# Input-projection evictions on ScalarE, adaLN units spread over row tiles, dense stages begun inside the norms, and changed orders at stage ends

## The chip, the cores and the metric

One core of a Trainium2 chip runs the whole program in one launch. The metric is the device time in microseconds (us) of one execution, as the median of several. Engines: TensorE (PE; weight loads are PEld), VectorE (DVE), ScalarE (ACT), GpSimd (POOL) and SyncE (SP), which here issues loads. Each engine runs its own program in order and waits on semaphores.

## What is computed

A two-layer backbone over 512 latent and 256 context rows (six row tiles of 128; NT = 6, LT = 4 latent tiles) of width 1024, in float32. Cut to what matters:

```python
for layer in range(2):                                   # 0 even, 1 odd
    mod = silu(c) @ ada_w[layer] + ada_b[layer]          # adaLN: 6 x 1024, for c and for c_ctx
    h = rms_norm(x, pre_mix_g) * (1 + mod[1]) + mod[0]
    p = h @ w_in                                         # even 1184 columns, odd 2560
    a, b = (mla(p), swa(p)) if layer == 0 else (na(p), gqa(p))   # some columns RMS-normed, some rotated
    x = x + mod[2] * rms_norm(concat(a, b) @ w_out, post_mix_g)
    h = rms_norm(x, pre_ffn_g) * (1 + mod[4]) + mod[3]
    gate, val = split(h @ ffn_up)                        # 2 x 2816 columns
    f = (gelu(conv3(gate)) * val) @ ffn_down
    x = x + mod[5] * rms_norm(f, post_ffn_g)
```

The context rows go through layer 0 wholly and through layer 1 only as keys and values.

## The kernel before, in words

**Products.** A float32 operand is split in a high part (ScalarE copies it to the rounded type, `split_hi`, L1159) and a low part (VectorE subtracts, `minus_hi`, L1424). Each product is three matmuls (`three`, L723 to 725; up projection L1056). Weights come in units: SP loads a unit into one of two raw slots, ScalarE and VectorE split it (`w_hi_done`, `w_lo_done`), PE uses it. Six PSUM banks hold accumulators, one per row tile; banks 6 and 7 are a ring that transposes (`turn`) and adaLN products share. `t_done`/`t_free` count its rounds, and a round waits until the one two before is emptied.

**Stages.** They follow one another: norm0, input projection in0 (72 to 228 us of the trace), MLA (`attention`, to 363), SWA (to 454), out0, norm1 (to 545), up0 (to 932), down0 (to 1112), norm2, in1 (to 1327), NA, GQA (to 1484), out1, norm3 (to 1553), up1 (to 1796), down1 (to 1929), norm4.

**Input projection** (PE L839, ACT `projection_splits` L1209, DVE L1653 with `chunk` L1579, POOL L1980). Two weight units per column chunk, all row tiles for each (`unit_mm`, L811). VectorE alone empties the banks (L1595) into four stage slots, squares the columns to be normed, scales and rotates them, and after each tile runs a tiny copy (`mark`, L1649) that lets POOL store the tile. In the even layer two adaLN units (256 columns of `ada_w`, 1 MB each, two raw slots, `ada_mm`) follow each weight unit, 16 in all; VectorE adds the four partial rows of each (`ada_evac`, L1430: L1437). PE waits for its load at L737. The latents of chunk 0 are turned in chunk 2. SP loads two adaLN units, then a weight unit, in turn (L624).

**Attention.** SP loads heads once `stages_stored` says the projection's tiles are in memory; VectorE waits for the same at step k == 0.

**Output projection** (PE L1018, ACT L1296). Two units; `out_order` has tiles 0 and 1 go through unit 0 first, the others through both at once. ScalarE splits both units and then copies and squares the first half of every bank (`first_half`, L1204).

**Norm** (ACT L1164, DVE L1526, POOL L1965). A loop over row tiles in four stages; VectorE releases a bank, makes the normed rows (L1509) and the low part of the turned rows (L1424). `late(0)` and `late(1)` split the next stage's first two weight units, at t == T and after the loop. PE turns each tile (`norm_turn` L785, `norm_turns` L793). Beside norm0 and norm2 PE runs the next projection's first unit tile by tile; beside norm1 and norm3 it only turns.

**Up projection** (PE L1038, ACT L1313, DVE L1804). 22 products of 96 matmuls, 128 gate and 128 value columns each, over banks 0 to 2 or 3 to 5. ScalarE and VectorE make the convolution, gelu and gate of a product and split the next unit. In layer 0 VectorE also multiplies a unit of layer 1's `ada_w` by both streams and sums it (`ada_multiply` L1468: L1478, L1481), PE sums that over partitions (`ada_across` L762, L767), and VectorE evacuates the row (`late_evac` L1443, L1449). 24 units go so: 22 in the up projection, unit 0 ahead of its first tile, two more in the down projection.

**Down projection** (PE L1073, ACT L1341, DVE L1843). Two column halves of eleven units. In the second half the last four (18, 20, 21, 19: `LATE_ORDER`) are done tile by tile, so that banks end one after another; units 20 and 21 are loaded after 19. POOL stores the table of relative-position biases (`toeplitz`, L2077) after the adaLN row of unit 21.

## Time and profile before

| | us |
|---|---|
| median of 3 runs (lowest, highest) | 1939.31 (1936.67, 1942.23) |
| the profiled execution, its own time | 1940.28 |
| its span, first to last instruction | 1938.6 |
| PE busy (x9850 matmuls) | 1736.3 (90%) |
| DVE, ACT, POOL busy | 1081.6, 598.9, 260.1 |
| chain that ended last: PE, DVE, DMA, ACT, issue | 70%, 13%, 5%, 4%, 4% |
| mean granted TensorE clock | 0.953 |
| store of the bias table (POOL, 3.8 MB), its queue's share, 975 to 1040 us | 37.1% |

Busy times overlap between engines. A share of the chain says what the end hung on. The stages lie one behind another, so that idle time of PE within one is read from that stage. In rows by time, the bracket holds the idle time before the instruction and what ended it.

### The profile page before, as it was taken

Reading aid. Unit: us, or ns where it says so; the run is one execution under the profiler, and the core shown is the slowest. Engines: PE = TensorE matmul, PEld = TensorE weight load, DVE = VectorE, ACT = ScalarE, POOL = GpSimd, SP = SyncE. Lnnn points to the kernel's source line nnn. Section 1 sums busy time; section 2 is a strip of 40 time slices with the busy share of each in tenths; the row PEclk is TensorE's granted clock in tenths of the full one; section 3 lists DMA queues with packets and bytes.
Section 4 is the critical chain, followed back from the end, with each engine's and each line's share of the span. In section 5 each row is a group of like instructions: output and inputs, shape, how many; then the busy total and the mean of one; then the engine's idle time right before and its main releaser. Section 6 shows DMA issues by size and latency. Waiting matters only on the chain.

```text
span 1938.6 us, 26920 instructions
## 1 busy us (share of the span) xinstructions
PE 1736.3 (90%) x9850; PEld 1378.1 (71%) x9850; DVE 1081.6 (56%) x2143; ACT 598.9 (31%) x941; POOL 260.1 (13%) x396
## 2 busy tenths in 40 slices
PE   5788599899889999999889978997989699999996
PEld 1667366567678888888667767885667578888785
DVE  3576555573667777777445473367743534443344
ACT  2201255562422211222224331113642333332342
POOL 0232223231200000000000020115521100000000
PEclk9899799999989999999999988998999899999998
DMA  8446923114333444334162533335502333332224
GB/s 288 140 163 225 242 44 87 25 26 131 122 107 103 124 130 129 105 114 130 65 132 80 179 124 131 115 113 133 134 19 84 123 87 87 108 87 76 76 98 141
DMA packets 258266, 224.15 MB, mean 116 GB/s; under 512 B 67484, under 2 KB 218411, under 8 KB 258178
## 3 DMA queue, kind: packets, MB, share of 16 engines
q1 hardware_dynamic: 249156, 202.50, 34.6%
q0 software_dynamic: 7008, 18.79, 3.3%
q10 hardware_dynamic: 2016, 1.71, 0.3%
q8 instruction: 54, 0.88, 0.2%
q14 instruction: 32, 0.26, 0.0%
HBM read 193.71 MB, written 29.25 MB: 115 GB/s over the span
## 4 chain that ended last, share of the span: by engine, by line
PE 70%; DVE 13%; DMA 5%; ACT 4%; issue 4%; POOL 2%; SPq 1%; DVEq 0%; ACTq 0%
PE ps L1056 32%; PE ps L723 7%; PE ps L724 7%; PE ps L725 7%; PE ps L900 5%; PE ps L982 4%; PE ps L945 4%; DMA w_raw<-in_ffn_down 2%; DVE act_lo L1424 1%; DVE w_lo L1424 1%; DVE late_row L1437 1%; DVE arena L1595 1%; PE ps L937 1%; PE ps L779 1%; DVE arena L1550 1%
## 5 line engine op out<-in xcount | busy, mean ns | idle before, releaser
L723 PE MATMUL ps<-w_hi,act_hi 128*128 128x512 f32 (+2 forms) x952 | 376.4, 395 | 45.2 <-DVE act_lo L1424 32.0
L1424 DVE TENSOR_TENSOR w_lo<-w_raw,w_hi 128x2048 fp32r<-128x2048 f32 (+3 forms) x114 | 209.5, 1839 | 299.0 <-ACT w_hi L1159 286.6
L724 PE MATMUL ps<-w_lo,act_hi 128*128 128x512 f32 (+2 forms) x952 | 372.8, 392 | 0.0
L725 PE MATMUL ps<-w_hi,act_lo 128*128 128x512 f32 (+2 forms) x952 | 372.6, 391 | 0.0
L1159 ACT ACTIVATE w_hi<-w_raw 128x2048 fp32r<-128x2048 f32 (+3 forms) x110 | 172.2, 1567 | 495.9 <-PE ps L725 352.0
L1056 PE MATMUL ps<-act_hi,w_hi 128*128 128x512 f32 (+1 forms) x1056 | 322.1, 359 | 2.8 <-DVE act_lo L1424 2.8
L1056 PE MATMUL ps<-act_lo,w_hi 128*128 128x512 f32 (+1 forms) x1056 | 322.9, 360 | 0.0
L1056 PE MATMUL ps<-act_hi,w_lo 128*128 128x512 f32 (+1 forms) x1056 | 319.6, 357 | 0.0
L723 PEld LDWEIGHTS ps<-w_hi,act_hi 128*128 128x128 f32 x952 | 185.4, 195 | 87.0 <-issue 40.7
L725 PEld LDWEIGHTS ps<-w_hi,act_lo 128*128 128x128 f32 x952 | 184.3, 194 | 35.9
L724 PEld LDWEIGHTS ps<-w_lo,act_hi 128*128 128x128 f32 x952 | 184.7, 194 | 34.7
L1056 PEld LDWEIGHTS ps<-act_hi,w_hi 128*128 128x128 f32 x1056 | 174.1, 189 | 37.9 <-issue 4.7
L1056 PEld LDWEIGHTS ps<-act_hi,w_lo 128*128 128x128 f32 x1056 | 176.2, 190 | 32.0
L1056 PEld LDWEIGHTS ps<-act_lo,w_hi 128*128 128x128 f32 x1056 | 175.2, 190 | 28.9
L900 PE MATMUL ps<-ident,arena 128*128 128x128 f32 x882 | 141.3, 290 | 28.4 <-ACT arena L1238 13.5
L900 PEld LDWEIGHTS ps<-ident,arena 128*128 128x128 f32 x882 | 97.2, 144 | 77.3 <-issue 30.5
L1326 ACT ACTIVATE arena<-ps,conv 128x768 f32<-128x768 f32 (+1 forms) x44 | 39.0, 886 | 345.2 <-PE ps L1056 319.1
L2055 POOL TENSOR_SCALAR arena<-arena,rinv 128x768 f32<-128x768 f32 (+3 forms) x144 | 111.6, 775 | 236.0 <-DVE rinv L1756 235.9
L1478 DVE SCALAR_TENSOR_TENSOR arena<-arena,silu 128x256 f32<-128x256 f32 x336 | 137.2, 479 | 0.9
L1255 ACT ACTIVATE arena<-arena,nb 128x768 f32<-128x768 f32 (+4 forms) x144 | 115.4, 801 | 28.1 <-DVE nb L1751 27.5
L1238 ACT ACTIVATE arena<-ps 128x384 f32<-128x384 f32 (+2 forms) x179 | 78.2, 437 | 143.9 <-PE ps L900 141.6
L1820 DVE SCALAR_TENSOR_TENSOR arena<-ps,conv,arena 128x511 f32<-128x511 f32 x66 | 41.6, 658 | 128.9 <-ACT arena L1326 128.9
(117 smaller groups left out, 1722.2 us busy)
## 6 DMA issues: line engine op xcount, KB each, us to landing
arena<-in_ada_w SPq DMA_DIRECT2D x44, 1024.0 KB, 9.5
w_raw<-in_ffn_up SPq DMA_DIRECT2D x88, 512.0 KB, 5.2
w_raw<-in_ffn_down SPq DMA_DIRECT2D x88, 256.0 KB, 2.9
w_raw<-in_odd_w_in SPq DMA_DIRECT2D x20, 512.0 KB, 4.6
arena<-mods SPq DMA_DIRECT2D x16, 512.0 KB, 7.2
proj_odd<-arena POOLq DMA_DIRECT2D x26, 256.0 KB, 2.4
x_after_mix<-arena SPq DMA_DIRECT2D x10, 512.0 KB, 2.9
arena<-x_after_mix SPq DMA_DIRECT2D x10, 512.0 KB, 4.3
```

The lines of the kernel that those rows point to most:

```text
L723: mm(out_, s_hi, m_hi, start=start, stop=False)
L724: mm(out_, s_hi, m_lo, start=False, stop=False)
L725: return mm(out_, s_lo, m_hi, start=False, stop=stop)
L900: last = nc.tensor.transpose(bank(b)[:, n * P:(n + 1) * P], src, ident[:, :])
L945: last = mm(out_of(x, off, n), qt[s][h, rows], kt[s][h, keys], start=True, stop=not rope)
L1056: last = mm(o, wt[:, k, :], m[:, k, rows], start=st, stop=sp_)
L1159: A(w_hi[:, s, 0:n], w_raw[:, s, 0:n], ACT.Copy).then_inc(w_hi_done, 1)
L1238: A(dst, bank(6, n * P), ACT.Copy).then_inc(left_free, 1)
L1255: A(dst, src, ACT.Exp, bias=nb[:, s, x:x + 1], scale=-1.0, accum_out=rsum[:, s, x:x + 1])\
L1424: V.tensor_sub(out_, full, hi.bitcast(fp32)).then_inc(sem_, 1)
L1478: ins = V.scalar_tensor_tensor(out=ada_sum[:, v, :], in0=w, scalar=x, in1=ada_sum[:, v, :], op0=ALU.mult, op1=ALU.add)
L2055: Q.tensor_scalar(v, v, rinv[:, k % 2, x:x + 1], 1.0, ALU.mult, ALU.mult).then_inc(p_scaled, 1)
```

## The change

Every engine's program is edited at the same seams.

- In both input projections ScalarE empties the banks (`evict`), squares included; VectorE only finishes tiles that are normed or rotated (`finish`), POOL stores the others straight from the stage slot; there are seven slots and no `mark`.
- The 16 adaLN units of in0 have three slots and go one at a time behind row tiles: `ADA_AT` maps (weight unit, tile) to them. SP issues weight units ahead of them.
- `first_half` in the output projections runs before the second split; the last two tiles of `out_order` go through unit 0 and then unit 1.
- In the norms the two late splits move to the start of iterations T-1 and T. PE does the first two up products in pieces of two row tiles (`rows_product`) between the turns, and both units of chunk 0 of in1 (`IN1_START`).
- In up0 `ada_multiply` runs at the end of a tile, unit 0 behind tile 0, and `ada_across` follows one product later. The last product does its low rows of weights first (`last_product`), so that the first half of G is split during it; down0's first unit takes banks by `up_banks`.
- In the down projections units 20 and 21 are loaded at the start of the second half and split before 17, 18 and 19; the first two and the last two tiles of the late units are interleaved.

Storage, placement and orders:

```diff
+STAGES = 7
...
-        stage = [plain(512) for _ in range(4)]
+        stage = [plain(512) for _ in range(4)] + [arena[:, 8704 + i * 512:9216 + i * 512] for i in range(3)]
+        early_raw = [ada_raw[:, 0], ada_raw[:, 1], arena[:, 4608:4608 + 2048].rearrange("p (k c) -> p k c", k=KC)]
...
+        ADA_AT = {(1, 5): [0, 1], (2, 1): [2], (2, 3): [3], (2, 5): [4], (3, 1): [5], (3, 3): [6], (3, 5): [7],
+                  (4, 5): [8], (5, 2): [9], (5, 5): [10], (6, 2): [11], (6, 5): [12], (6, 8): [13], (6, 11): [14],
+                  (7, 3): [15]}
+        TURN0 = 8
...
-        LATE_ORDER = [18, 20, 21, 19]
-        SPLIT_PLACE = {18: 20, 19: 21, 20: 18, 21: 19}
+        SPLIT_PLACE = {20: 17, 21: 18, 17: 19, 18: 20, 19: 21}
+        def late_order(T):
+            first = [(t, n) for t in range(2) for n in (20, 21, 18)] + [(t, 19) for t in range(2)]
+            middle = [(t, n) for t in range(2, T - 2) for n in (18, 20, 21, 19)]
+            return first + middle + [(t, n) for pair in ((18, 20), (21, 19)) for t in (T - 2, T - 1) for n in pair]
...
+            first, last = ([(t, n) for n in range(2) for t in ts] for ts in ((0, 1), (T - 2, T - 1)))
+            return first + [(t, n) for t in range(2, T - 2) for n in range(2)] + last
...
+        IN1_START = [("turn", 3), (0, 0), (0, 1), (0, 2), (1, 0), ("turn", 4), (1, 1), (1, 2), ("turn", 5), (0, 3), (1, 3)]
```

SyncE's loads (`early_unit(i)` loads adaLN unit i of the projection into slot i % 3 once unit i - 3 is summed); in the down projection `half` is the second half:

```diff
+                            sp.wait_ge(t_free, ada_round(0, ADA_FIRST + 14) + 1)
...
-            for n in range(8):
-                for g in range(ADA_FIRST + 2 * n, ADA_FIRST + 2 * n + 2):
-                    sp.wait_ge(t_free, ada_round(0, g - 2) + 1 if g - 2 >= ADA_FIRST else WIDES)
-                    ada_unit(0, g, g % 2)
-                k_unit(n + 2, *units[n + 2])
+            sp.wait_ge(t_free, WIDES)
+            for i in range(2):
+                early_unit(i)
+            for n in (2, 3):
+                k_unit(n, *units[n])
+            sp.wait_ge(h_ready, base("norm0", "h") + NT)
+            early_unit(2)
+            for n, late in ((4, (3, 4)), (5, (5, 6, 7)), (6, (8, 9)), (7, (10, 11)), (8, (12, 13)), (9, (14, 15))):
+                k_unit(n, *units[n])
+                for i in late:
+                    early_unit(i)
...
-                        if layer == 0:
-                            wait_apart(sp, (t_free, i * 2 + (base(up, "t") + k + 1)))
-                            ada_unit(1, i * 2 + (k + 2), k)
-                run_loop(sp, 0, FT // 2 - 1, up_trip)
+                        if layer == 0 and not (isinstance(i, int) and i == k == 0):
+                            wait_apart(sp, (t_free, i * 2 + (base(up, "t") + k)))
...
+                    if half:
+                        sp.wait_ge(w_lo_done, w0 - 1)
+                        for n in (20, 21):
+                            down_unit(layer, 2 * (n - FT // 2), half, n % 2, 1024)
...
+                        sp.wait_ge(t_free, ada_round(1, FT - 3) + 1)
+                        ada_unit(1, FT - 1, 1)
                         for k in range(2):
+                            run_loop(sp, 1 + 2 * k, 3 + 2 * k, down_trip)
                             sp.wait_ge(t_free, ada_round(1, FT - 2 + k) + 1)
                             ada_unit(1, FT + k, k)
-                            run_loop(sp, 1 + 2 * k, 3 + 2 * k, down_trip)
```

TensorE:

```diff
+            def into_projection():
+                u = base("in1", "w")
+                for what, t in IN1_START:
+                    if what == "turn":
+                        norm_turn("norm2", t)
+                        continue
+                    weights(u + what)
+                    turned("norm2", t)
...
+                            if u == 4:
                                 pe.wait_ge(staged, b + 1)
-                                turn(t0 + 8 + b, t0 + 8 + b,
+                                turn(t0 + TURN0 + b, t0 + TURN0 + b,
                                      [mla_in[b][:, k * P:(k + 1) * P] for k in range(3)])
-                        unit_mm(u % 2, tiles, 4, cn, (act_hi, act_lo), 4 * n, n == 0, n == 1, after=after)
...
+                def rows_product(j, g):
+                    weights(U0 + j)
+                    for t in (2 * g, 2 * g + 1):
+                        turned(nm, t)
+                    for half in range(2):
+                        b = 3 * j + 2 * half if g < 2 else 3 * j + 1
+                        o = bank(b, 256, 256 * g) if g < 2 else bank(b, CTX, CTX * half)
+                        if b < T:
+                            pe.wait_ge(acc_evac, base(name, "ev") - T + b + 1)
+                        for k in range(KC):
+                            cols = slice(half * 1024 + k * P, half * 1024 + (k + 1) * P)
+                            last = three_moving(o, w_hi[:, j, cols], w_lo[:, j, cols],
+                                                *(m[:, k, g * 256:(g + 1) * 256] for m in (act_hi, act_lo)),
+                                                k == 0, k == KC - 1)
+                        if g == T // 2 - 1:
+                            last.then_inc(mm_done, 1)
...
+                def last_product(slot):
...
+                    b = 3 * slot
+                    for half in range(2):
+                        last = passes(half, range(KC // 2), bank(b + 2 * half), slice(0, LAT))
+                    if full:
+                        for half in range(2):
+                            last = passes(half, range(KC), bank(b + 1, CTX, CTX * half), slice(LAT, ROWS))
+                    last.then_inc(low_free, 1)
+                    for half in range(2):
+                        passes(half, range(KC // 2, KC), bank(b + 2 * half), slice(0, LAT)).then_inc(mm_done, 1)
...
-                    if full:
-                        ada_across(i * 2 + (base(name, "t") + k), k, i * 2 + (k + 1))
...
+                    if full and not ends:
+                        ada_across(i * 2 + (base(name, "t") + k - 1), 1 - k, i * 2 + k)
...
+                todo = [(j, g) for g in range(T // 2) for j in range(2)]
+                for t in range(T - 3, T):
+                    if T == NT:
+                        rows_product(*todo.pop(0))
+                    norm_turn(nm, t)
+                    if T == LT and t > T - 3:
+                        rows_product(*todo.pop(0))
+                for j, g in todo:
+                    rows_product(j, g)
+                if full:
+                    ada_across(base(name, "t"), 0, 1)
+                run_loop(pe, 1, FT // 2 - 1, lambda i: [tile(i, k, True) for k in range(2)])
+                tile(FT // 2 - 1, 0, True)
+                tile(FT // 2 - 1, 1, True, True)
...
+                def up_banks(b):
+                    if b in (0, 3):
+                        pe.wait_ge(gated, base(name, "f") - (b == 0))
...
+                        order = late_order(len(tiles))
+                        for i, (t, n) in enumerate(order):
+                            done = ends(order, t) == i + 1
+                            late(t, n, done)
+                            if nf == "norm2" and t >= 3 and done:
                                 norm_turn(nf, t - 3)
```

ScalarE (norm, input projection, output projection, last tile of the up projection, down projection):

```diff
-                    if t == T and late is not None:
-                        late(0)
+                    if T - 1 <= t <= T and late is not None:
+                        late(t - T + 1)
...
+                    other = 0 if c >= 3 and layer == 0 or n % 2 else 1 if layer and c == 0 else len(tiles)
+                    act.wait_ge(mm_done, in_done(layer, c, len(tiles) - 1) - other)
...
+                def evict(c):
+                    spec = IN_SPECS[layer][c]
+                    n = spec["n"]
+                    for x, t in enumerate(in_tiles(layer, c)):
+                        ev, st, _, nsq = in_counts(layer, c, x)
+                        act.wait_ge(mm_done, in_done(layer, c, x))
...
+                            last = A(scrap[:, off:off + w], bank(x)[:, at:at + w], ACT.Square, accum_out=ssh[:, p, k:k + 1])
...
+                            at_least(act, stage_out[st % STAGES], 16 * (st // STAGES))
+                            dst = stage[st % STAGES][:, 0:n]
+                        A(dst, bank(x, n), ACT.Copy).then_inc(acc_evac, 1)
...
+                    split(2 * c)
+                    if layer and c == 0:
+                        for s in range(2):
+                            act.wait_ge(x_st[s], 16 * base("in1", "xs") // 2)
+                    evict(c)
+                    split(2 * c + 1)
...
+                    if n:
+                        for t in range(T):
+                            act.wait_ge(mm_done, mm0 + T + t + 1)
+                            first_half(t)
...
-                act.wait_ge(mm_done, base(name, "mm"))
...
+                        act.wait_ge(low_free, layer + 1)
+                        for n in range(2):
+                            A(act_hi[:, 2 * n:2 * n + 2, 0:cols], G[:, 2 * n:2 * n + 2, 0:cols], ACT.Copy).then_inc(g_hi, 1)
...
+                if layer == 0:
+                    act.wait_ge(ada_summed, ADA_UNITS)
```

VectorE (norm, attention, up projection and its last tile, down projection):

```diff
+                    if T - 1 <= t <= T and late is not None:
+                        late(t - T + 1)
...
-                    if k == 0 and a.name in ("mla", "na"):
+                    if k < 0 and a.name in ("mla", "na"):
...
-                if full:
-                    ada_multiply(0, ADA_USES + 1)
...
-                        late_evac(i * 2 + (T0 + k), k, i + (ADA_USES + 1))
-                        ada_multiply(1 - k, i + (ADA_USES + 1 + k))
...
+                        if not (isinstance(i, int) and i == k == 0):
+                            late_evac(i * 2 + (T0 + k - 1), 1 - k, i + (ADA_USES + k))
+                        if ada == 1:
+                            ada_multiply(k, i + (ADA_USES + 1))
...
+                        for n in range(2):
+                            dve.wait_ge(g_hi, base(f"down{layer}", "g") + n + 1)
+                            chunks = slice(2 * n, 2 * n + 2)
+                            minus_hi(act_lo[:, chunks, 0:cols], G[:, chunks, 0:cols], act_hi[:, chunks, 0:cols], g_lo)
+                    tile(FT // 2 - 1, k, 1024, 2 * full if k == 0 else 0)
...
+                    ada_multiply(0, ADA_USES + FT // 2)
...
+                for first, last, g in ((0, 1, FT - 1), (1, 3, FT), (3, 4, None)):
+                    run_loop(dve, first, last, lambda i: [step(i, k, 0, 0) for k in range(2)])
+                    if g is not None:
+                        ada_turn(g)
```

GpSimd, in the input projection:

```diff
+                    if on_vector(layer, c, t):
+                        pool.wait_ge(staged, done + 1)
+                    else:
+                        pool.wait_ge(acc_evac, ev + 1)
```

## Rows read from the trace of the kernel before

**Rows 1.** Busy time by stage, all engines; us, (x) instructions

```profile
core 0: us, PE busy (x) PEld busy (x) DVE busy (x) ACT busy (x) POOL busy (x), PEclk, DMA share, GB/s
112.00:228.00 116.00, 84.56 (x564) 67.39 (x562) 79.38 (x203) 11.44 (x12) 26.29 (x49) 0.91 0.70 228
...
518.00:545.00 27.00, 15.22 (x73) 12.02 (x71) 22.37 (x25) 12.37 (x22) 4.11 (x11) 0.74 0.61 195
...
545.00:932.00 387.00, 386.38 (x2280) 327.66 (x2280) 278.61 (x585) 78.61 (x65) 11.44 (x21) 0.99 0.38 113
```

**Rows 2.** Waits of PE, 80 to 229 us: us in total, times, longest

```profile
PE ps L737 <- DMA late_bias<-in_ada_b: 14.9, 5, 6.3
...
PE ps L723 <- DVE arena L1595: 12.2, 5, 5.6
...
PE ps L900 <- DVE late_row L1437: 9.6, 1, 9.6
```

**Rows 3.** VectorE groups, 80 to 228 us; busy us, mean ns, idle before

```profile
L1437 DVE TENSOR_TENSOR late_row<-ps,late_row 2x256 f32<-2x256 f32 x48 | 20.2, 420 | 1.6
...
L1595 DVE COPY arena<-ps 128x512 f32<-128x512 f32 x18 | 12.4, 690 | 8.0 <-DMA mla_kv<-arena 7.8
```

**Rows 4.** ScalarE groups, 228 to 545 us; same columns

```profile
L1199 ACT ACTIVATE act_hi<-ps 128x512 fp32r<-128x512 f32 x12 | 6.9, 596 | 8.9 <-PE ps L779 8.9
```

**Rows 5.** Busy time in one 5 us stretch; columns of rows 1

```profile
130.00:135.00 5.00, 5.00 (x24) 4.14 (x23) 4.83 (x10) 0.00 (x0) 1.06 (x2) 1.00 1.04 344
```

**Rows 6.** PE by time, second pass of the first output projection

```profile
489.89 0.61 PE L723 MATMUL ps<-w_hi,act_hi 128*128 128x512 f32 x1 [3.18 <-ACT ps L1207]
```

**Rows 7.** PE by time, transposes at the end of the first post-mix norm

```profile
533.82 1.94 PE L779 MATMUL ps<-ident,arena 128*128 128x128 f32 x8 [4.85 <-DVE act_lo L1424]
```

**Rows 8.** Chain by time, first two up-projection products; start, us, what

```profile
545.62 19.60 PE ps L1056 x96
...
565.55 17.16 PE ps L1056 x96
```

**Rows 9.** VectorE by time, first two up-projection tiles

```profile
571.65 2.29 DVE L1424 TENSOR_TENSOR w_lo<-w_raw,w_hi 128x2048 fp32r<-128x2048 f32 x1 [0.55 <-ACT w_hi L1159]
...
575.60 5.75 DVE L1478 SCALAR_TENSOR_TENSOR arena<-arena,silu 128x256 f32<-128x256 f32 x14
...
589.15 2.29 DVE L1424 TENSOR_TENSOR w_lo<-w_raw,w_hi 128x2048 fp32r<-128x2048 f32 x1 [0.57 <-ACT w_hi L1159]
...
592.57 0.62 DVE L1481 TENSOR_SCALAR arena<-arena,silu 128x256 f32<-128x256 f32 x2
...
593.10 5.76 DVE L1478 SCALAR_TENSOR_TENSOR arena<-arena,silu 128x256 f32<-128x256 f32 x14
```

**Rows 10.** PE by time, even down projection

```profile
941.24 0.77 PE L723 MATMUL ps<-w_hi,act_hi 128*128 128x512 f32 x1 [8.79 <-DVE act_lo L1424]
...
987.61 0.40 PE L767 MATMUL ps<-arena,ones 128*1 128x128 f32 x8 [3.97 <-DVE arena L1478]
...
1018.84 0.57 PE L723 MATMUL ps<-w_hi,act_hi 128*128 128x512 f32 x1 [4.49 <-DVE act_lo L1424]
...
1107.47 0.47 PE L723 MATMUL ps<-w_hi,act_hi 128*128 128x512 f32 x1 [3.06 <-DVE act_lo L1424]
```

**Rows 11.** Chain by time, even down projection

```profile
1001.36 22.58 DMA w_raw<-in_ffn_down
```

**Rows 12.** DMA issues (page, part 6): KB each, median us from issue to landing

```profile
w_raw<-in_ffn_down SPq DMA_DIRECT2D x88, 256.0 KB, 2.9
```

**Rows 13.** VectorE by time, before the norm after it

```profile
1118.11 1.23 DVE L1462 SCALAR_TENSOR_TENSOR arena<-arena 128x1024 f32<-128x1024 f32 x1 [7.98 <-DMA arena<-in_pre_mix_g]
```

**Rows 14.** PE by time, odd input projection's start

```profile
1135.19 1.97 PE L779 MATMUL ps<-ident,arena 128*128 128x128 f32 x8 [4.10 <-DVE arena L1509]
...
1184.61 0.77 PE L723 MATMUL ps<-w_hi,act_hi 128*128 128x512 f32 x1 [4.96 <-DVE w_lo L1424]
```

**Rows 15.** PE by time, odd layer: norm, down projection, last units

```profile
1541.23 1.94 PE L779 MATMUL ps<-ident,arena 128*128 128x128 f32 x8 [7.04 <-DVE act_lo L1424]
...
1798.97 0.77 PE L723 MATMUL ps<-w_hi,act_hi 128*128 128x512 f32 x1 [3.74 <-DVE act_lo L1424]
...
1905.79 0.77 PE L723 MATMUL ps<-w_hi,act_hi 128*128 128x512 f32 x1 [6.20 <-DVE act_lo L1424]
```

588 lines of the change are left out of this document (286 added, 302 removed).

## Prediction

> **What bounds the kernel now.** I read the stages first. TensorE (PE) is busy nearly all the time in the even up projection (386.38 of 387 us) but not in the even input projection (84.56 of 116 us) or at the end of the first post-mix norm (15.22 of 27 us) [rows 1]. No other engine is near its limit: VectorE has 79.38 us of work in the 116, ScalarE 11.44 [rows 1]. So the time is PE's work plus PE's idle stretches, and the change is read stretch by stretch: what PE waits for there, and what waits last once that is gone. Next I read the waits of PE in the input projection: five on the loads of adaLN weights, 14.9 us; five on the bank evictions (line 1595), 12.2; one on the last adaLN row at attention's start, 9.6 [rows 2]. Last I read PE by time in the other stages. An idle stretch costs more than itself: the first up-projection product after the norm takes 19.60 us, the next 17.16 [rows 8], and the granted clock of the 27 us before is 0.74 [rows 1]. I add 1.0 to 2.4 us after an idle stretch of over 3 us and nothing after a shorter one.
>
> The sum is made against the profiled execution, 1940.3 us (its span is 1938.6); the median of the runs, 1939.3, is 1 us lower, which I leave out.
>
> **Input projection, even layer.** VectorE's 18 evictions of 512 columns (12.4 us) and the others move to ScalarE, which has the room. The price there: 596 ns for 128x512 from PSUM [rows 4] against VectorE's 690 [rows 3]. "ScalarE: Activation LUTs" of the Trainium skill (Rules for kernel authors) says to keep such simple operations on VectorE and budgets 0.3 us plus 0.83 ns an element for an activation; that is an estimate of 0.72 us and would make 26 such evictions 3 us longer than by the row, off the path as long as ScalarE is idle; the trace does not agree, and the sum goes by the row. The adaLN units no longer come in pairs after a weight unit but singly behind row tiles, three weight slots ahead; each costs VectorE four additions, 16 units x 4, the same as before (48 of them 20.2 us, [rows 3]). Placed by hand in the new order, PE runs from 86 us with waits of 1 to 2 us and ends its last tile near 178 instead of 219; SP then still issues the loads for attention one after another, and the first scores come about 40 us sooner. The 36.7 us of waits [rows 2] plus some 4 us of slow clock are there to be won. Against that stand the transfers: 116 us at 228 GB/s are 26.4 MB [rows 1], and the highest rate in view, 344 GB/s at a share of 1.04 [rows 5], moves them in 77 us, so this stretch can give 39 us at most and the 7.8 us of idle ahead of it a little more. I take **38**; bounds 27 (the loads' and evictions' waits alone) and 47. The wait for all stores is now ahead of the first score minimum instead of after it; VectorE, and with it the softmax of both first attentions, stands behind it. The stores land before the first scores are there, so it costs 0 (up to +3 at either attention).
>
> **Output projections.** ScalarE now empties each bank as it is finished instead of after the last split. PE's 3.18 us at 489.89 [rows 6] and the same wait in the odd layer go, with 0.7 and 1.4 of slow clock: **8.5**. The split of the second unit is then behind four to six evictions; PE has two tiles, over 5 us, before it needs it, so 0 to +1.
>
> **First norm into the up projection.** PE waits 4.85 us at 533.82 and twice more [rows 7]; the first product starts at 545.62 and the second ends at 582.7 [rows 8]. The six half-sized pieces are together the same 34.3 us and can begin once unit 0's low part is made. But VectorE now makes it (2.29 us, [rows 9]) ahead of the last tile's norm, which delays the turned rows by as much. By hand: pieces from 531.5, with three transposes between them, the last of product 0 done at 564, of product 1 at 569.5. That alone would be 13 us. Then PE meets the adaLN sum of unit 0. Before, VectorE made it ahead of the first tile; now behind it: product 0's end to unit 2's low part is 8.7 us (565.2 to 573.9), and 14 of the 16 multiply-adds are 5.75 us, so all about 6.5 [rows 8, 9]. PE is released 15.2 us after 564, at 579.2, and the third product begins there instead of at 583, with 2 us of slow clock: **2**. Bounds: -3 (if the norm slips more) and +13 (if that sum hid).
>
> **Up into down, even layer.** 8.79 us idle [rows 10]. Two of the four row chunks of the first unit are split before the last product ends, and the first three of six tiles need only the banks of the tile before. PE does about 4 us, waits 1.5 for the last gate, does the rest, and again waits for an adaLN sum that VectorE makes behind the last tile: some 3.5 us. **4.5** (0 to 10). In the middle, the 3.97 us on that sum [rows 10] go with their slow clock, 5.5. The 22.58 us landing of a weight load [rows 11], with the 4.49 us stall after it [rows 10], comes from the store of the bias table beside it. That store now starts later, among the loads of the second half, which have two units more in front. "DMA: Bandwidth & Descriptors" (SWDGE vs HWDGE vs iDMA) of the Trainium skill says an engine takes turns between the two kinds of queue; by that the load would only take about twice its 2.9 us [rows 12] and the stall be none, so that the middle would give 2.5 more than my term; the trace has 22.58, and I keep the stall and charge 2.5 for the worse place: **3** (-6 to +12).
>
> **Second norm into the odd input projection.** The 3.06 us before the last units [rows 10] go, but the norm cannot start until the gain row is loaded after the last split (7.98 us on that load, [rows 13]), so the stall at 1135.19 (4.10, [rows 14]) grows by as much. What is won comes after: tile 5's products end sooner, PE works on both halves of chunk 0 inside the norm, and the 4.96 us at 1184.61 [rows 14] fill up. By hand, chunk 0 ends at 1188 instead of 1197: **9** (0 to 14). At the end of the odd projection VectorE no longer lags by its own copies and squares: **3** (0 to 4).
>
> **Third norm into up.** Only four row tiles. PE waits 7.04 us at 1541.23 [rows 15]. Unit 0's low part now goes ahead of tile 3, the transposes queue behind the same two banks, and both products end together instead of 11 us apart, so unit 2's split starts late: third product at 1581.5 instead of 1577.6, **-4** (-6 to +8). **Odd down projection:** 3.74 us at 1798.97 with slow clock, **5**; 6.20 us at 1905.79 with slow clock, as the units 20 and 21 are loaded early, **8** of 21.8 us of last units (4 to 9) [rows 15].
>
> **Sum:** 38 + 8.5 + 2 + 4.5 + 3 + 9 + 3 - 4 + 5 + 8 = 77 us; 1940.3 - 77 = **1863**.
>
> **Rivals.** (A) The overlap in the norms is really won. For: PE's order allows it, and of 11 us at both up projections I give nearly all back to waits that I placed by hand. Against: rows 9. Then 13 instead of 2 and +3 instead of -4, and a calmer middle: 1843. Chance 0.2. (B) The input projection stays bound by transfers: average share 0.70 already [rows 1], saturated stretches [rows 5]. Then only some 20 us come there: 1881. Chance 0.2. (C) The overlaps fail and the store of the bias table stops the second half too; only the plain removals stay: 1900. Chance 0.05. (D) Slower. In the up loop of the even layer PE's adaLN product of unit n is now behind product n+1 and needs a sum that VectorE ends 16.3 us after product n: the second product ends at 582.7, unit 3's low part at 591.44, the row evacuation of 1.2 follows, and the multiply takes from 592.57 to 598.86 [rows 8, 9]; PE comes 17.2 us after product n [rows 8]. Each us by which VectorE runs over that 0.9 is paid in 19 periods, with slow clock on top. It decides from 4.5 us over (19 x 4.5 is 86 us, more than the 75 won elsewhere); at 5 us over, 1958. For it: VectorE is busy 278.61 of 387 us there [rows 1] with nearly all in one chain. Against it: the chain's parts are the same, only turned. Chance 0.03. (E) ScalarE in the input projection is held by its waits in program order, the splits queue behind evictions, and nothing comes there: the rest gives 39, 1901. Chance 0.04. The forecast keeps 0.48.
>
> **Range.** 1842 to 1889 holds forecast, A and B with their bounds (independent terms of 2 to 12 us make about 14 around each); C, D, E and the fringes are 0.2. About 0.3% (6 us) is what a measurement of this kernel can tell from no change. Faster 0.95, same 0.02, slower 0.03.
>
> **What would show it.** Right: PE idle in 86 to 180 us under 10 us, first scores near 195 instead of 235; a PE wait of 8 to 10 us on VectorE's multiply line ahead of the third product in up0; one of 3 to 4 us behind the first down unit; a wait of 7 us at the first transposes of the second norm; a store of the bias table beside late second-half loads; odd up projection's third product no sooner relative to its norm. Wrong: the input projection still with waits on adaLN loads of over 15 us; a period of over 17.6 us in the up loop; no wait ahead of the third product.

## The result, and the profile after

The changed kernel takes 1858.11 us (median of four runs, 1856.10 to 1860.17) against 1939.03 us before (four runs); the ratio is 0.9582, with a 95% interval from 0.9562 to 0.9601. The forecast was 1863, range 1842 to 1889. The profiled execution has a span of 1854.4 us, against 1938.6.

Page of the changed kernel, busy time and the chain that ended last:

```profile
PE 1706.3 (92%) x10042; PEld 1366.3 (74%) x10042; DVE 1019.9 (55%) x1927; ACT 645.6 (35%) x1089; POOL 267.3 (14%) x396
...
PE 80%; DVE 6%; DMA 4%; ACT 3%; issue 3%; SPq 2%; POOL 2%; ACTq 0%; DVEq 0%
```

The span fell by 84.2 us. TensorE's busy time fell by 30.0 of them (1736.3 to 1706.3), although it now has 192 matmuls more: the mean granted clock rose from 0.953 to 0.972. The old busy time at the new clock would be 1736.3 x 0.953 / 0.972 = 1702 us, so that the clock accounts for it. The other 54 us are idle time of PE. VectorE's part of the chain went from 13% to 6%.

Busy time by stretch, changed kernel (columns of [rows 1]); the first is the even input projection up to its last tile, the second its late part with what follows up to the transposes of MLA, the others the even up projection behind its first products, and the even down projection:

```profile
86.00:178.00 92.00, 89.58 (x650) 70.25 (x643) 60.43 (x144) 28.24 (x47) 29.18 (x57) 1.00 0.80 263
...
112.00:188.00 76.00, 65.50 (x503) 52.65 (x501) 48.06 (x117) 28.91 (x48) 25.29 (x47) 0.98 0.90 291
...
533.00:884.00 351.00, 351.00 (x2076) 297.79 (x2077) 252.90 (x525) 74.29 (x62) 10.89 (x20) 1.00 0.41 118
884.00:1060.00 176.00, 157.11 (x699) 127.59 (x698) 92.43 (x127) 57.38 (x61) 6.06 (x8) 0.95 0.44 116
```

The transfers now fill 0.90 of the engines in what is left of the stretch of [rows 1], against 0.70 there. The even down projection kept its idle time: 18.9 us of 176 now, 21.8 of 180 before (932 to 1112 us).

Waits of PE, changed kernel, 60 to 200 us; they answer to [rows 2], where the first row was 14.9, the bank evictions 12.2 and the last adaLN row 9.6:

```profile
PE ps L993 <- DMA arena<-mla_kv: 8.2, 1, 8.2
PE ps L821 <- DMA late_bias<-in_ada_b: 2.4, 1, 2.4
PE ps L1038 <- DVE nb L1866: 2.1, 1, 2.1
```

PE by time, changed kernel: first transposes of norm0, transposes of MLA that wait for the loaded keys and values, then the adaLN sum behind the first two up products, down projection, second and third norm:

```profile
44.22 1.75 PE L863 MATMUL ps<-ident,arena 128*128 128x128 f32 x8 [3.44 <-DVE arena L1700]
...
188.08 4.15 PE L993 MATMUL ps<-ident,arena 128*128 128x128 f32 x18 [8.16 <-DMA arena<-mla_kv]
...
532.32 0.61 PE L851 MATMUL ps<-arena,ones 128*1 128x128 f32 x8 [9.14 <-DVE arena L1669]
...
889.09 0.47 PE L806 MATMUL ps<-w_hi,act_hi 128*128 128x512 f32 x1 [1.55 <-DVE arena L1944]
...
896.43 0.40 PE L851 MATMUL ps<-arena,ones 128*1 128x128 f32 x8 [2.98 <-DVE arena L1669]
...
996.11 0.77 PE L806 MATMUL ps<-w_hi,act_hi 128*128 128x512 f32 x1 [14.36 <-DVE act_lo L1614]
...
1085.86 1.97 PE L863 MATMUL ps<-ident,arena 128*128 128x128 f32 x8 [8.67 <-DVE arena L1700]
...
1475.79 1.94 PE L863 MATMUL ps<-ident,arena 128*128 128x128 f32 x8 [9.26 <-DVE act_lo L1614]
```

Set beside [rows 10, 14, 15]: the 8.79 us ahead of the even down projection became 1.55 and 2.98; the 3.06 ahead of its last units and both waits of the odd down projection are gone, and the 4.96 in the odd input projection became 1.66. Three grew: 4.10 to 8.67 at the second norm, 7.04 to 9.26 at the third, and 4.49 to 14.36 in the even down projection. One is new, 9.14 us for the adaLN sum.

How far the changed kernel is ahead at marks that both traces have. ScalarE's first pass over a product marks its end in the even layer; in the odd layer it waits for the gate columns only, so that it marks the middle of a product, in both kernels alike. ScalarE by time, the third and the 21st product of the even up projection and the third of the odd one, kernel before:

```profile
600.38 0.99 ACT L1326 ACTIVATE arena<-ps,conv 128x768 f32<-128x768 f32 x1 [11.27 <-PE ps L1056]
...
914.86 0.99 ACT L1326 ACTIVATE arena<-ps,conv 128x768 f32<-128x768 f32 x1 [11.03 <-PE ps L1056]
...
1583.57 0.78 ACT L1326 ACTIVATE arena<-ps,conv 128x512 f32<-128x512 f32 x1 [3.98 <-PE ps L1056]
```

The same in the changed kernel:

```profile
551.99 0.99 ACT L1515 ACTIVATE arena<-ps,conv 128x768 f32<-128x768 f32 x1 [14.91 <-PE ps L1171]
...
866.45 0.99 ACT L1515 ACTIVATE arena<-ps,conv 128x768 f32<-128x768 f32 x1 [11.03 <-PE ps L1171]
...
1514.07 0.78 ACT L1515 ACTIVATE arena<-ps,conv 128x512 f32<-128x512 f32 x1 [3.30 <-PE ps L1171]
```

| up to this mark | ahead, us | won since the last | forecast |
|---|---|---|---|
| first transposes of norm0 (45.99, 44.22) | 1.8 | 1.8 | 0 |
| second scores of MLA (239.37, 197.40) | 42.0 | 40.2 | 38 |
| start of the first output projection | 42.4 | 0.4 | 0 |
| third product, even up projection | 48.4 | 6.0 | 3.9 + 2 |
| 21st product | 48.4 | 0.0 | 0 |
| first transposes of norm2 (1135.19, 1085.86) | 49.3 | 0.9 | 4.5 + 3 |
| second scores of NA (1333.17, 1270.32) | 62.9 | 13.5 | 9 + 3 |
| start of the second output projection | 62.9 | 0.0 | 0 |
| third product, odd up projection | 69.5 | 6.6 | 4.6 - 4 |
| end | 84.2 | 14.7 | 5 + 8 |

(The 8.5 us for the output projections is split as 3.18 + 0.7 and 3.18 + 1.4.) Ahead of the even up projection one profiled execution differs from another by up to some 7 us whatever the edit: the first transposes come at 43.6 to 46.9 us over the twelve kernels below and the two above, on loads of the adaLN prelude, and the stretch from them to MLA's scores has a scatter of its own. Experiments 7 and 8, whose programs are those of the changed kernel up to there, reach the third even product 4.8 and 5.0 us behind it. Further on there is one such place: from the second output projection to the third odd product the changed kernel takes 92.6 us, and all ten others with this stretch unchanged 93.9 to 94.4. So the experiments are read by stretch, and their medians only for what is larger.

### The profile page after: what moved, and what is told of

Same layout as the page of the kernel before. It is cut to its first block, busy times and chain, and to the rows that moved or that the text cites. A ratio compares the mean times of both kernels' runs of the same rounds, so it can differ in the third digit from the quotient of the medians.

```text
span 1854.4 us, 27146 instructions
## 1 busy us (share of the span) xinstructions
PE 1706.3 (92%) x10042; PEld 1366.3 (74%) x10042; DVE 1019.9 (55%) x1927; ACT 645.6 (35%) x1089; POOL 267.3 (14%) x396
## 4 chain that ended last, share of the span: by engine, by line
PE 80%; DVE 6%; DMA 4%; ACT 3%; issue 3%; SPq 2%; POOL 2%; ACTq 0%; DVEq 0%
PE ps L1171 29%; PE ps L806 10%; PE ps L808 10%; PE ps L807 10%; PE ps L993 5%; PE ps L1075 4%; PE ps L1038 4%; PE ps L1181 1%; DMA w_raw<-in_ffn_down 1%; PE ps L1030 1%; PE ps L863 1%; PE ps L1045 1%; ACT arena L1425 1%; PE ps L1155 1%; DMA wide_raw<-in_ada_w 1%
## 5 line engine op out<-in xcount | busy, mean ns | idle before, releaser
L806 PE MATMUL ps<-w_hi,act_hi 128*128 128x512 f32 (+2 forms) x952 | 370.1, 389 | 21.8 <-DVE act_lo L1614 18.6
L808 PE MATMUL ps<-w_hi,act_lo 128*128 128x512 f32 (+2 forms) x952 | 366.2, 385 | 0.0
L807 PE MATMUL ps<-w_lo,act_hi 128*128 128x512 f32 (+2 forms) x952 | 366.2, 385 | 0.0
L1171 PE MATMUL ps<-act_lo,w_hi 128*128 128x512 f32 (+1 forms) x912 | 278.3, 359 | 0.0
L1171 PE MATMUL ps<-act_hi,w_hi 128*128 128x512 f32 (+1 forms) x912 | 277.1, 358 | 0.0
L1171 PE MATMUL ps<-act_hi,w_lo 128*128 128x512 f32 (+1 forms) x912 | 274.6, 355 | 0.0
L806 PEld LDWEIGHTS ps<-w_hi,act_hi 128*128 128x128 f32 x952 | 180.9, 190 | 62.1 <-issue 23.3
L1171 PEld LDWEIGHTS ps<-act_hi,w_lo 128*128 128x128 f32 x912 | 151.5, 189 | 27.8
L1171 PEld LDWEIGHTS ps<-act_hi,w_hi 128*128 128x128 f32 x912 | 149.4, 188 | 29.7 <-issue 4.5
L1171 PEld LDWEIGHTS ps<-act_lo,w_hi 128*128 128x128 f32 x912 | 150.7, 189 | 24.6
```

The costliest lines, as they stand in the source:

```text
L806: mm(out_, s_hi, m_hi, start=start, stop=False)
L807: mm(out_, s_hi, m_lo, start=False, stop=False)
L808: return mm(out_, s_lo, m_hi, start=False, stop=stop)
L1171: last = mm(o, wt[:, k, :], m[:, k, rows], start=st, stop=sp_)
```

## The experiments

**1 and 2. Where the store of the bias table stands.** Edit, in the changed kernel and in the one before; GpSimd's block from the memset of `rpb` to the store moves as it is:

```diff
             attention("mla", MLA)
+            own.inc(Q.memset(rpb[:, :], 0.0))
...
             attention("swa", SWA)
             norm("norm1")
...
-            own.inc(Q.memset(rpb[:, :], 0.0))
```

> The changed kernel with GpSimd's store of the bias table moved from behind the up projection to between the two attentions of the even layer. Theory T (the 14.36 us stall of TensorE in the even down projection is this store taking the transfer engines from the weight loads of the second half): the stall is under 1.5 us, no weight load of that stage takes over 8 us, every later stage comes 14 to 16 us sooner, at most 3 us are lost at the start of the second attention, and the time is 1843 (1840 to 1848). Rival R (the loads are late because SyncE issues a 1 MB adaLN unit and two extra weight units ahead of them): a stall of over 8 us stays there and the time is 1855 to 1860.

> The same move of the store in the kernel before. Theory T: the load of 22.58 us and the stall of 4.49 us behind it go, with about 1 us of slow clock, and nothing else moves: 1933 (1931 to 1936). Together with the run on the changed kernel this gives what the change made the store cost more: 14.4 against 4.5 us, some 10 us. Rival R: no difference, 1939.

Measured: 1849.67 us (ratio 0.9529, 0.9511 to 0.9548) and 1935.53 us (0.9975, 0.9960 to 0.9989). The chain and the waits of PE in the second half of the even down projection; changed kernel, 960 to 1075 us:

```profile
967.14 24.54 DMA w_raw<-in_ffn_down
```

```profile
PE ps L806 <- DVE act_lo L1614: 14.4, 1, 14.4
```

The waits with the store moved, same window (the one that is left is norm2's):

```profile
PE ps L863 <- DVE arena L1700: 8.0, 1, 8.0
```

Theory T holds, R falls. From the 21st product of the even up projection to the third of the odd one, moving the store wins 16.4 us in the changed kernel (from 6.3 behind to 10.2 ahead of it) and 10.1 in the kernel before (0.5 behind to 9.6 ahead). Six kernels in which the stretch is unchanged have it within 0.6 us, experiment 9 has it 3 us shorter. So the store cost 10 us before, not the 5.5 that its one stall suggested, and the change made it 6.4 us dearer. The size of the whole was missed in the first (1849.67 against 1840 to 1848): the new place costs 3.3 us (1.65 in the second attention, as much in the output projection), 3.2 us of scatter lie ahead of that and 1.8 at the very end, so that 8.4 us are left in the median. The 1.8 us are no scatter: behind the start of VectorE's last instruction the program takes 8.7 to 9.3 us in all three kernels whose store is moved, and 6.9 to 7.0 in the eleven others; no row says why. In the kernel before the whole comes to 7.6 us in the profiled executions and to 5 in the medians, a ratio so near 1 that the times alone would not show it.

**3. The adaLN sum of unit 0 first.**

```diff
+                if full:
+                    ada_multiply(0, ADA_USES + 1)
+
                 def tile(i, k, size, ada=int(full)):
...
-                    tile(0, k, 2048)
+                    tile(0, k, 2048, full * k)
```

> The changed kernel with VectorE's multiply of adaLN unit 0 put back ahead of the first up-projection tile of the even layer; everything else stays. Theory (the 9.14 us wait of TensorE for this sum is all that gives back the overlap of norm and first two products; VectorE stands idle for 11.23 us ahead of that tile, and the multiply takes 6.4): the wait goes, the third product then waits for the low part of its weights until about 526.6 instead of 532.9, all that follows is 6 us sooner, 1852 (1850 to 1855). Rival (the multiply delays the last turned rows, or the weights' low part is as late as the sum): 0 to 2 us, 1856 to 1858.

Measured: 1852.28 us (0.9545, 0.9514 to 0.9575). PE by time, ahead of the third product:

```profile
525.62 1.00 PE L1171 MATMUL ps<-act_hi,w_hi 128*128 128x512 f32 x2 [2.52 <-DVE w_lo L1614]
```

In place of 9.14 us on the sum PE waits 2.52 on the weights' low part. The third product ends at 544.72 instead of 551.99, 7.3 us sooner, of which 0.4 were there at the first product; the rest of the program keeps it. The theory holds; the change gave back 7 us of its overlap for no need. The 7 us are one profiled execution against another; the four runs of this kernel lie between 1847 and 1857 us.

**4. No products inside the post-mix norms.**

```diff
                 for t in range(T - 3, T):
-                    if T == NT:
-                        rows_product(*todo.pop(0))
                     norm_turn(nm, t)
-                    if T == LT and t > T - 3:
-                        rows_product(*todo.pop(0))
```

> The changed kernel with TensorE turning all row tiles of both post-mix norms before the six (four) pieces of the first two up products. Theory (the pieces run inside the norm save TensorE time, and the wait for the adaLN sum only follows product 0 at a fixed distance, so a later product 0 makes a later third product): in the even layer the pieces start at about 494.8 instead of 483.9 and the third product begins 7 us later; in the odd layer they start 1 us later; 1866 (1863 to 1868). Rival (the wait on the sum hides it, so that the overlap is worth nothing): the third product is no later, 1858.

Measured: 1874.71 us (0.9644, 0.9618 to 0.9671). PE by time, this kernel, the last two turns it waits for and the sum:

```profile
495.98 1.94 PE L863 MATMUL ps<-ident,arena 128*128 128x128 f32 x8 [5.85 <-DVE act_lo L1610]
501.83 1.94 PE L863 MATMUL ps<-ident,arena 128*128 128x128 f32 x8 [3.91 <-DVE act_lo L1610]
...
551.36 0.61 PE L851 MATMUL ps<-arena,ones 128*1 128x128 f32 x8 [9.15 <-DVE arena L1665]
```

From the first turn that PE waits for in this norm (488.46, against 481.17 in the changed kernel) to the sum it takes 62.9 us instead of 51.15: 11.7 us more in the even layer, and 2.1 in the odd one. The rival falls: PE waits 9.15 us for the sum as before, behind a later product, since the sum is made a fixed time after product 0. The theory's size was too small: the pieces begin at 506.01, which is 22.1 us after 483.88, 7.3 of it scatter ahead of the norm, so 14.8 and not 10.9, since the last turns wait for their predecessors' low parts. The time is outside the 1863 to 1868 that had been stated.

**5, 6 and 9. The even input projection taken apart.** Edits (placement in pairs; VectorE's copies of the chunks that are not normed):

```diff
-        ADA_AT = {(1, 5): [0, 1], (2, 1): [2], (2, 3): [3], (2, 5): [4], (3, 1): [5], (3, 3): [6], (3, 5): [7],
...
+        ADA_AT = {(1, 5): [0, 1, 2, 3], (2, 5): [4, 5], (3, 5): [6, 7], (4, 5): [8, 9], (5, 5): [10, 11],
+                  (6, 11): [12, 13], (7, 11): [14, 15]}
```

```diff
+                        if not spec["norms"]:
+                            continue
                         act.wait_ge(mm_done, in_done(layer, c, x))
...
+                            dve.wait_ge(mm_done, in_done(layer, c, x))
+                            at_least(dve, stage_out[st % STAGES], 16 * (st // STAGES))
+                            dve.wait_ge(acc_evac, ev)
+                            V.tensor_copy(stage[st % STAGES][:, 0:n], bank(x, n)).then_inc(acc_evac, 1)
...
```

> The changed kernel with the adaLN units of the even input projection behind the last row tile of a weight unit again (four behind the first, then two and two), with three slots and ScalarE's evictions kept. Theory (spreading is what lets the 1 MB loads hide: behind the first weight unit the fourth adaLN unit can only be loaded once the first is summed): TensorE waits on adaLN loads some 6 us there and 1 to 3 us at each later pair, attention's first transposes come 8 to 14 us later, 1868 (1865 to 1873). Rival (three slots and SyncE's new order are enough, the placement is worth nothing): under 2 us, 1858 to 1860.

> The changed kernel with VectorE copying the banks of all column chunks that are not normed (24 of 30 tiles of the even projection, 14 of 24 of the odd one); seven slots and spread adaLN units kept. Theory (VectorE has no room for the copies beside adaLN sums and rotations): waits of TensorE on that copy in the last chunks of the even projection, 5 to 12 us there as in the kernel before, and 3 us ahead of the odd layer's first attention, in all 1868 (1864 to 1873). Rival (before, the copies were late only since the adaLN units came in pairs): under 2 us in each layer, 1858 to 1861.

> Both of the earlier edits to the even input projection at once in the changed kernel: adaLN units in pairs again and VectorE's copies of the chunks that are not normed (the pairs alone cost 12 us from first transposes to first scores, the copies alone about 2). Theory (the two help each other: behind a pair VectorE has eight additions ahead of the next copy, so that banks are emptied late): 18 us or more there, 1880 (1874 to 1888). Rival (they are independent): 12 to 15 us, 1872 to 1875.

**10 and 11. Its slots.**

```diff
-STAGES = 7
+STAGES = 4
```

```diff
-                if i >= 3:
-                    sp.wait_ge(t_free, ada_round(0, g - 3) + 1)
+                if i >= 2:
+                    sp.wait_ge(t_free, ada_round(0, g - 2) + 1)
```

> The changed kernel with four stage slots in place of seven. Theory (before, VectorE's copies waited for stores of the stage slots, 8 us in the row of the copies, and PE for the copies): ScalarE waits for stores in the last two column groups of the even projection and TensorE 3 to 8 us behind it, nothing in the odd one, 1865 (1862 to 1869). Rival (with ScalarE as the evicting engine the slots turn round in time): under 1.5 us, 1859 to 1861.

> The changed kernel with the load of each of the 16 early adaLN units waiting for the unit two before it to be summed, not three. Theory (a 1 MB unit takes about 10 us to land and TensorE comes to the next every 6 to 8 us, so that only the third slot hides the load): waits on adaLN loads of 2 to 4 us at most units, 15 us in all (8 to 30), 1875 (1867 to 1890). Rival (placing the units apart is enough, the third slot is spare): under 3 us, 1859 to 1862.

The five are read by the stretch from norm0's first transposes to those of MLA that wait for the loads (44.22 and 188.08 above; before, MLA's transposes are one block at 228.42). Seven kernels whose input projection is that of the changed kernel have 143.9 to 146.6 us, mean 145.3.

| kernel | stretch, us | against 145.3 | median, us (ratio, interval) |
|---|---|---|---|
| before | 182.4 | +37.1 | 1939.03 |
| 5, pairs | 157.8 | +12.5 | 1871.85 (0.9646, 0.9629 to 0.9663) |
| 6, VectorE copies | 147.8 | +2.5 | 1865.71 (0.9614, 0.9598 to 0.9630) |
| 9, both | 160.3 | +15.0 | 1875.72 (0.9667, 0.9644 to 0.9689) |
| 10, four stage slots | 147.3 | +2.0 | 1861.55 (0.9594, 0.9572 to 0.9617) |
| 11, two adaLN slots | 155.3 | +10.0 | 1869.07 (0.9636, 0.9610 to 0.9662) |

Waits of PE, 60 to 229 us, with pairs (5):

```profile
PE ps L820 <- DMA late_bias<-in_ada_b: 5.3, 2, 3.8
PE ps L992 <- DMA arena<-proj_even: 5.2, 1, 5.2
PE ps L820 <- DVE late_row L1626: 5.0, 1, 5.0
```

With VectorE's copies (6), and with both (9):

```profile
PE ps L806 <- DVE arena L1808: 1.7, 2, 1.4
```

```profile
PE ps L805 <- DVE arena L1807: 6.1, 4, 5.4
PE ps L992 <- DVE late_row L1628: 5.2, 1, 5.2
PE ps L820 <- DVE late_row L1628: 5.0, 1, 5.0
```

With four stage slots (10), and two adaLN slots (11):

```profile
PE ps L806 <- ACT arena L1395: 2.4, 2, 1.3
```

```profile
PE ps L821 <- DMA late_bias<-in_ada_b: 10.6, 4, 5.0
```

What the change is named after, eviction on ScalarE, brings 2.5 us there as long as the adaLN units stand apart (1.2 us beyond the highest of the seven; measured to MLA's second scores it is within their scatter), and nothing in the odd layer: from 1143.10 to 1266.35 it takes 123.25 us, exactly as in the changed kernel (1139.45 to 1262.70). The medians have more, 0.9614 against 0.9582 or 6 us, with intervals that just overlap; no row of the trace has the other 4, and runs of one kernel differ by as much, so that 2.5 us is the better reading and not a bound. That holds for the copies of the chunks that are not normed; ScalarE kept those with squares, and moving those back was not tried. For 6 the time lies in the range of the theory, but its waits of 5 to 12 us are not there (1.7 us) nor its 3 us in the odd layer, so the theory falls; the rival's "under 2 us" is near, not met. Placement brings 12.5, the third slot 10.0, and here the medians agree (12 and 10 by the ratios). For 9 the rival holds: 15.0 is 12.5 + 2.5, so that the two are independent; yet the wait on copies did come back behind pairs (6.1 us against 1.7) without making the stretch longer than the sum; that it is hidden by what was late anyhow is not shown. For 10 the rows show what the theory named, in a size under it (2.4 us on evictions); its rival's bound of 1.5 is not clearly passed, so that one stays open. Placement, third slot, copies and stage slots make 27 of the 37 us if they add up, which was tried for one pair only; the other 10 (SyncE's order, the copies and squares of chunk 0, the tiny copies) were not taken apart.

**7. The last up product in the usual order.**

```diff
-                    if ends:
-                        last_product(k)
-                    else:
-                        product(0, k)
-                        product(1, k)
+                    product(0, k)
+                    product(1, k)
```

ScalarE's and VectorE's splits of the first four row chunks move behind the last gate.

> The changed kernel with the last product of both up projections in the usual order and the first four row chunks of G split behind the last gate. Theory (my terms of 4.5 and 5 us for the two seams are this split): TensorE stands idle 8 to 9 us ahead of the even down projection and 3 to 4 us ahead of the odd one, 4 and 4 us later than in the changed kernel with slow clock, 1867 (1864 to 1869). Rival (in the even layer the wait on the adaLN sum behind the first unit is there anyhow and takes it all): only the odd layer loses, 1862.

Measured: 1872.74 us (0.9645, 0.9622 to 0.9668). PE by time, the starts of the two down projections:

```profile
897.15 0.76 PE L806 MATMUL ps<-w_hi,act_hi 128*128 128x512 f32 x1 [8.63 <-issue]
...
1741.15 0.47 PE L806 MATMUL ps<-w_hi,act_hi 128*128 128x512 f32 x1 [3.59 <-issue]
```

Beyond what it lagged ahead of the seam, 7.0 us are lost at the even seam (4.8 to 11.8 behind) and 5.5 at the odd one (11.8 to 17.3). The waits are those of [rows 10, 15]; the theory holds and its sizes were low by 3 and 1.5. The rival falls. The time is outside the 1864 to 1869 that had been stated.

**8. The last four units tile by tile.**

```diff
+            return [(t, n) for t in range(T) for n in (20, 21, 18, 19)]
```

> The changed kernel with the last four units of both down projections tile by tile, in the order 20, 21, 18, 19, with their early loads and splits kept. Theory (the early loads bring what the end of the down projections gained; interleaving only covers the splits of 18 and 19): a wait of 1 to 2 us at the first tile's unit 19 in either layer and nothing else, 1861 (1859 to 1863). Rival (interleaving is what pays): waits of 3 to 6 us as in the kernel before and 1866 or more.

Measured: 1864.36 us (0.9612, 0.9593 to 0.9631). No wait at a tile's unit 19 in either layer, where the theory had 1 to 2 us. From the 21st even product to the third odd one it loses 3.5 us, 1.6 of them by the end of norm2. Against the changed kernel the rest lies behind the second output projection, where that kernel's own execution is the odd one out by 1.7 us (above); against the others it lies ahead of it. So it is not located, and in the even layer the interleaving may be worth up to 3.5 us. The odd layer's end loses nothing (8.3 us behind at its products and 8.3 at the end): there the early loads, not the order, removed the 6.20 us of [rows 15], and the theory holds. The time is between those of theory (to 1863) and rival (from 1866).

**12. A version from these.** Experiment 3's edit, and the store in pieces:

```diff
+            for g in range(10):
+                ada_store(1, T0 + g, g % 2, g)
+                if g >= 2:
+                    rows = slice(15 * (g - 2), 15 * (g - 1))
+                    pool.dma_start(toeplitz[rows, :].rearrange("r (c x) -> r c x", x=TZ_W),
...
-                    sp.wait_ge(tz_out, 16)
+                    sp.wait_ge(tz_out, 128)
```

> A version made from what the runs showed: the changed kernel with VectorE's multiply of adaLN unit 0 ahead of the first up tile, and with the store of the bias table cut in eight pieces of 15 rows, one behind each of the adaLN units 2 to 9 in the even up projection, where the transfer engines are mostly idle. Theory (the store costs 16 us of the changed kernel where it stands, the sum 7, and a piece of half a megabyte fits into one product's 17.4 us without making a weight load late): period of the up loop unchanged at 17.4 us, no stall over 1.5 us in the second half of the even down projection, 1836 (1832 to 1841). Rival (pieces make weight loads late in the up loop, where TensorE has no slack): products of over 18 us in that stretch, 1843 or more.

Measured: 1853.89 us (five runs; 0.9552, 0.9533 to 0.9571), no better than the whole store in attention (1849.67 without the early sum). The rival holds. PE by time in the up loop:

```profile
623.18 0.40 PE L851 MATMUL ps<-arena,ones 128*1 128x128 f32 x8 [2.66 <-DVE arena L1669]
...
680.13 0.40 PE L851 MATMUL ps<-arena,ones 128*1 128x128 f32 x8 [1.74 <-DVE arena L1669]
```

DMA issues, 549 to 740 us (KB each, median us to landing):

```profile
w_raw<-in_ffn_up SPq DMA_DIRECT2D x20, 512.0 KB, 9.9
toeplitz<-rpb POOLq DMA_DIRECT2D x8, 476.2 KB, 9.9
```

The same row of the changed kernel, 543 to 734 us:

```profile
w_raw<-in_ffn_up SPq DMA_DIRECT2D x21, 512.0 KB, 6.3
```

Loads land 3.6 us later, and VectorE's chain, which has next to no slack in the period, passes that on: the lead over the changed kernel goes from +1.0 us at the fifth product to -10.1 at the 14th, over the eight pieces (578.9 to 711.7 us), with periods of up to 21.7 us. It is +4.5 at the third odd product, without the stall of the down projection, and 2.2 at the end. My premise that idle transfer engines make a place free was wrong: VectorE waits 28.9 us for ScalarE's split of the weights there (560 to 760 us), and 6.8 in the changed kernel. The place that counts is one where no chain waits for a load. The whole store in attention together with experiment 3 should do better (an estimate from experiments 1 and 3, 1858 - 16.4 + 3.3 + 1.8 - 6.9 = 1840 us); it was not run.

## Why the prediction was right, and where not

The total was right (77 us of gain forecast, 81 in the medians, 84 in the profiled executions), and most terms by their own steps. In part it was luck: two terms missed by some 4 to 7 us each, with opposite signs, and cancel.

- **Input projection, even layer**: 38 forecast, 40.2 to the second scores. PE's idle time in it is 2.4 us (92.00 less 89.58), and the transfers' share of 0.90 from 112 us on shows rival B close. The bound of 39 us by transfers was not what held, though: the 76 us move 22.1 MB at 291 GB/s and not 26.4, while the 40 us ahead of it (72 to 112) move 152 GB/s now against 82 before, and the 7.8 us that PE stood idle in them are gone. But the step "evictions move to ScalarE, which has the room" carries about 2.5 us only; 5 and 11 show that placement and the third slot carry the stretch, and 9 that with pairs the copies wait again (6.1 us of the 12.2 [rows 2]). ScalarE's evictions of 128x512 took 598 ns (row below), 596 in [rows 4]. The 0.72 us of the prediction come from the budget that "ScalarE: Activation LUTs" of the Trainium skill (Rules for kernel authors) states for an activation whose bias is a pointer operand. These copies have no bias operand, so that the rows do not speak against the page; the prediction left its condition out. The first scores came at 192.90, "near 195". The last wait is now 8.16 us of PE for a load that SyncE issues once the stores have landed. VectorE's moved wait costs nothing: PE waits 2.1 us for its score minimum ahead of the second scores, and 1.93 before.

ScalarE's groups, changed kernel, 62 to 190 us (columns of [rows 3]):

```profile
L1395 ACT ACTIVATE arena<-ps 128x512 f32<-128x512 f32 x18 | 10.8, 598 | 21.2 <-PE ps L808 19.3 <-DMA mla_kv<-arena 1.2
```

- **Output projections**: 3.18 us gone twice, as forecast.
- **First norm into up**: forecast 3.9 + 2, measured 6.0. The wait came where it was placed, 9.14 us against "8 to 10". Experiment 3 shows it as the cause, 4 what the overlap is worth with it, and rival A as partly right about what could be had: 7 us more, so 9 in all beside the 3.9, where A had 13.
- **Rival D**, the up loop of VectorE's chain longer than PE's period: the lead is 48.4 us at the third and at the 21st product, so no period grew. Falls. (By its rows the sum ends 16.2 us after the product, not 16.3, which leaves 1.0 us of slack and not 0.9.)
- **Up into down, even layer**: 4.5 forecast, 7.0 by experiment 7, so the term was too small, within its bounds of 0 to 10. Since the stretch from the 21st product to the second norm gained 0.9 us in all, the middle lost some 6 where 3 were forecast, the edge of its bounds (the 3.97 went, the stall of the store grew by 9.87). The 3.97 us in the middle went and 2.98 came behind unit 1, as "some 3.5" was put there.
- **The store of the bias table**: the step that failed. "I keep the stall and charge 2.5 for the worse place": the stall went from 4.49 to 14.36 us, and the worse place cost 6.4 us more by experiments 1 and 2, where 2.5 had been charged. Rival C had this, with every overlap failing beside it, which did not happen. The prediction's other figure for this place is wrong in its sum: without stall and charge the middle would give 4.49 + 2.5, so 7 us more than the term, not 2.5. The load beside the store took 24.54 us against a median of 3.0 for that kind, and it was not the only one. DMA issues of the changed kernel, 960 to 1000 us:

```profile
w_raw<-in_ffn_down SPq DMA_DIRECT2D x9, 256.0 KB, 23.1
```

By the turns that an engine takes between the two kinds of queue, as "DMA: Bandwidth & Descriptors" of the Trainium skill (SWDGE vs HWDGE vs iDMA) has it, the prediction came to about twice 2.9 us. The trace does not show whether turns are taken; it shows that twice is no bound on what a load sees beside a 3.8 MB store.

- **Second norm into the odd projection**: 12 forecast, 13.5 measured, with the wait of 8.67 us at the first transposes ("7"). 9.1 of them are there at NA's first scores (1323.19, 1264.73). The other 4.4 come at the second, where PE waited 7.05 us for VectorE's minimum and now waits 2.65. The prediction's reason for its 3, VectorE's own copies and squares, is not shown: with the copies back (experiment 6) the wait is 2.91, and the squares were not moved.
- **Third norm into up**: the other step that failed, -4 forecast, +2 measured (6.6 less 4.6), or +0.3 if the stretch is taken as the ten other kernels have it. "Both products end together": they end 5.8 us apart, product 1 at 1508.1, and the low part of unit 2 is there at 1506.85. So it is there before PE has ended product 1; PE starts the third product at 1507.97 without a wait, and nothing was lost. Experiment 4 gives the overlap 2.1 us there. ScalarE by time, changed kernel, its first passes over products 0 and 1 (gate columns, in the middle of each last piece):

```profile
1499.61 0.78 ACT L1515 ACTIVATE arena<-ps,conv 128x512 f32<-128x512 f32 x1 [8.07 <-issue]
...
1505.38 0.78 ACT L1515 ACTIVATE arena<-ps,conv 128x512 f32<-128x512 f32 x1 [0.85 <-PE ps L1157]
```

VectorE by time, the low part:

```profile
1504.56 2.29 DVE L1614 TENSOR_TENSOR w_lo<-w_raw,w_hi 128x2048 fp32r<-128x2048 f32 x1 [1.11 <-ACT w_hi L1316]
```

- **Odd down projection**: 13 forecast, 14.7 measured, 5.5 of it the seam.

## What to carry to other kernels

When a stage is bound by loads and bank evictions at once, first ask what is queued ahead of the late work: here placing 16 small jobs singly was worth 12.5 us and one more slot 10.0, each taken back by itself, and the faster evicting engine 2.5. Before an overlap is credited, walk to the next thing that the same engine must finish; here one multiply of 6.4 us, placed behind a tile, left 6.0 of the 12.9 us that output projection, norm and first products had to give (experiment 3). A large store belongs where no chain waits for a load, and its price is to be measured by moving it, since its one visible stall showed half of it; the new place has a price too, here 5 of the 16 us.

## What had not been expected of the hardware

- A 256 KB load beside the 3.8 MB store lands after 24.54 us, and 22.58 before; in the changed kernel the nine of 960 to 1000 us have a median of 23.1, and with the store moved those of the same time have 3.0; eight stores of 476 KB, issued over 133 us, still raise the median of 512 KB loads from 6.3 to 9.9 us.
- Of the 84.2 us won, 30.0 are busy time of PE, with more matmuls than before, and go with a mean granted clock of 0.972 in place of 0.953. In the even input projection the clock is 1.00 now (86 to 178 us) where it was 0.91 [rows 1], and PE has next to no idle time there: where idle stretches go, the work itself gets shorter too.
- Executions with the same program up to there differ by 2.8 us in the input projection (143.9 to 146.6 us) and by 2 us from MLA's transposes to its second scores (9.3 to 9.7, or 11.3 to 11.4 us). What decides it is open.
- In the three kernels whose store is moved the program's end, behind the start of VectorE's last instruction, takes 8.7 to 9.3 us, and 6.9 to 7.0 in the eleven others. Why is open.
